# Retention's swapped halves and mLSTM's spread maximum: transfers on Pool's queue in place of matrix products

## What is computed

```python
x1, x2 = xf[..., :half], xf[..., half:]
return jnp.concatenate([x1 * cos - x2 * sin, x1 * sin + x2 * cos], axis=-1)
```

```python
m_t = jnp.maximum(jnp.max(Dlog, axis=2), inter)
W = jnp.exp(Dlog - m_t[:, :, None, :])
s = jnp.einsum('blhd,bshd->blsh', qc, kc) * W
```

## Time and profile before

| | |
|---|---|
| three runs | 1510.20, 1513.43 (median), 1519.79 us |
| span of the profiled execution | 1509.3 us |
| PE busy | 98% |
| DVE, ACT, POOL busy | 51%, 23%, 4% |
| PE clock granted | 0.9 or more of full in all 40 slices |
| DMA, mean | 199 GB/s; near full share in the last third (experts) |

### The profile page before, as it was taken

How to read it: one execution, slowest core, us unless ns; L and a number is a source line. 1 busy time by engine, 2 the same in 40 slices (tenths; PEclk the granted TensorE clock), 3 DMA queues, 4 the chain that set the end, 5 groups by cost and what they waited for, 6 DMA issues and landing times.

```text
span 1509.3 us, 40728 instructions
## 1 busy us (share of the span) xinstructions
PE 1479.3 (98%) x17933; PEld 1265.3 (84%) x17933; DVE 770.5 (51%) x1700; ACT 342.1 (23%) x855; POOL 56.2 (4%) x68
## 2 busy tenths in 40 slices
PE   9999999999999999999999999999999899999997
PEld 6899976887899999998899977887888787888654
DVE  6446756746665655657366667636662211221123
ACT  2314224222212212233224224123130000000001
POOL 1000010110000000000000010200010000000000
PEclk9999999999999999999999999999999999999999
DMA  8324435203544354256524353114879998999993
GB/s 349 115 88 164 155 139 133 85 25 93 210 154 153 131 188 144 81 207 225 201 100 176 144 150 111 45 44 125 330 314 359 407 360 304 361 355 366 363 385 106
DMA packets 64335, 299.84 MB, mean 199 GB/s; under 512 B 21840, under 2 KB 23568, under 8 KB 37664
## 3 DMA queue, kind: packets, MB, share of 16 engines
q1 hardware_dynamic: 50392, 268.10, 48.5%
q0 software_dynamic: 2944, 18.09, 3.1%
q10 hardware_dynamic: 10823, 11.05, 2.7%
HBM read 277.93 MB, written 19.28 MB: 197 GB/s over the span
## 4 chain that ended last, share of the span: by engine, by line
PE 93%; DVE 3%; DMA 2%; issue 1%; ACT 1%; SPq 0%; DVEq 0%; ACTq 0%
PE ps L2112 15%; PE ps L1250 12%; PE ps L1913 12%; PE ps L1713 9%; PE ps L2035 7%; PE ps L1720 5%; PE ps L1199 4%; PE ps L1825 4%; PE ps L2009 3%; PE ps L1212 2%; PE ps L1787 2%; PE ps L1569 2%; DMA ring<-in_mix 2%; PE ps L1946 2%; PE ps L1265 1%
## 5 line engine op out<-in xcount | busy, mean ns | idle before, releaser
L1713 PE MATMUL ps<-xn,ring 128*128 128x288 f32 x576 | 155.7, 414 | 0.4 <-ACT gate L2478 0.4
L1713 PEld LDWEIGHTS ps<-xn,ring 128*128 128x128 f32 x576 | 105.9, 190 | 37.2 <-issue 10.3
L2112 PE MATMUL ps<-arena 128*128 128x144 f32 x1028 | 133.4, 286 | 1.2 <-DVE arena L3649 1.2
L2112 PEld LDWEIGHTS ps<-arena 128*128 128x128 f32 x1028 | 129.3, 190 | 1.4 <-issue 1.4
L1913 PE MATMUL ps<-y_ml,arena 128*64 128x96 f32 (+4 forms) x2688 | 111.7, 244 | 11.5 <-issue 11.4
L1913 PEld LDWEIGHTS ps<-y_ml,arena 128*64 128x64 f32 x2688 | 109.2, 137 | 15.2 <-issue 15.1
L2035 PE MATMUL ps<-arena,mixed 128*32 128x256 f32 x2024 | 111.3, 380 | 0.0
L2035 PEld LDWEIGHTS ps<-arena,mixed 128*32 128x32 f32 x2024 | 65.0, 110 | 42.3 <-issue 0.2
L3573 DVE TENSOR_TENSOR mixed<-ps,mixed 128x96 f32<-128x96 f32 (+4 forms) x66 | 16.8, 254 | 130.3 <-PE ps L1913 130.1
L1913 PEld LDWEIGHTS ps<-y_ml,ring 128*64 128x64 f32 x1536 | 62.1, 137 | 4.8 <-issue 4.8
L1913 PE MATMUL ps<-y_ml,ring 128*64 128x96 f32 (+4 forms) x1536 | 64.3, 245 | 0.6 <-issue 0.6
(11 more groups left out here) (588 smaller groups left out, 2554.4 us busy)
## 6 DMA issues: line engine op xcount, KB each, us to landing
arena<-in_egu SPq DMA_DIRECT2D x56, 1024.0 KB, 7.4
ring<-in_mix SPq DMA_DIRECT2D x46, 1024.0 KB, 5.5
arena<-in_edown SPq DMA_DIRECT2D x40, 1024.0 KB, 7.3
ring<-in_mix SPq DMA_DIRECT2D x48, 768.0 KB, 4.2
ring<-in_egu SPq DMA_DIRECT2D x32, 1024.0 KB, 7.5
ring<-in_gu SPq DMA_DIRECT2D x14, 1024.0 KB, 4.8
arena<-in_gu SPq DMA_DIRECT2D x8, 1024.0 KB, 5.1
arena<-in_C POOLq DMA_DIRECT2D x2, 2048.0 KB, 7.9
```

Source lines behind the costliest of these rows:

```text
L1713: last = mm(ps[:, bank, 0:T], ring[:, s, P * k:P * k + P], xn[:, k, :], start=(k == 0), stop=(k == KT - 1))
L2112: last = mm(ps[:, dense_bank(side, product), 0:HALF], left, right, start=(k == 0 and product in (1, 2, 5)), stop=(k == n - 1), skip_group_ ...
```

## The change

The two kinds of product leave PE. The swapped halves come by four DMA transfers, each of 32 partitions with four tiles of 288 (`rqk` to `r_turned`), the running maximum by four DMA transfers that each read one partition's 256 numbers 128 times (`rows` to `row_copies`). All eight stand on Pool's queue, per layer. The copies of the rows wait for `lf_ok`; the swapped halves wait for the finished queries and keys and for PE's last head (`ml_nd` 4), since they are written over the mLSTM queries. n0 and the eight transfers share one semaphore: DVE waits for n0 and all four row copies at once, ahead of L2877, and for the four swaps ahead of the sine product, which is now one instruction of 1152 elements.

```diff
+        row_copies = at(19050, NH, TP)
+        r_turned = at(6570, 4, T)
+        ld_copies = sig("n0_and_copies_loaded", 144)
+        ld_n0_rows, ld_turned = Part(ld_copies, 79), Part(ld_copies, 143)
...
-                mm(ps[:, 4, 0:TP], picked_head(h), rows[0:NH, 1, 0:TP], start=True, stop=True)
                 mm(ps[:, 5, 0:TP], picked_head(h), rows[0:NH, 2, 0:TP], start=True, stop=True).then_inc(ml_bc.sem, 1)
...
-            def retention_rotate(l):
-                pe.wait_ge(*couple_added(l, 1, C12))
-                pe.wait_ge(*couple_copied(l, 1, 4))
-                for j in range(4):
-                    mm(ps[:, 4 + j, 0:T], C("swap", P), rqk[:, j, :], start=True, stop=True).then_inc(r_sw.sem, 1)
...
-                dve.wait_ge(ld_n0.sem, 16 * (l + 1))
+                dve.wait_ge(*ld_n0_rows(l))
...
-                STT(ml_W[:, 0:P], ps[:, 4, 0:P], g[0], C("causal_neg", P), ADD, ADD)
-                TSC(ml_W[:, P:TP], ps[:, 4, P:TP], g[0], None, ADD)
-                STT(ml_W[:, TP:PW], ps[:, 4, P:TP], g[1], C("causal_neg", P), ADD, ADD).then_inc(ml_wl.sem, 1)
+                STT(ml_W[:, 0:P], row_copies[:, h, 0:P], g[0], C("causal_neg", P), ADD, ADD)
+                TSC(ml_W[:, P:TP], row_copies[:, h, P:TP], g[0], None, ADD)
+                STT(ml_W[:, TP:PW], row_copies[:, h, P:TP], g[1], C("causal_neg", P), ADD, ADD).then_inc(ml_wl.sem, 1)
...
-                for j in range(4):
-                    dve.wait_ge(*r_sw(l, j + 1))
-                    last = TT(rt[:, j, :], ps[:, 4 + j, 0:T], C("sin", T), MUL)
-                link(last)
+                dve.wait_ge(*ld_turned(l))
+                link(TT(rt, r_turned, mid(C("sin", T), 4), MUL))
...
+                pool.wait_ge(*lf_ok(l))
+                for h in range(NH):
+                    pool.dma_start(row_copies[:, h, :], rows[h:h + 1, 1, 0:TP].unsqueeze(1).broadcast_to([1, P, TP])).then_inc(ld_copies.sem, 16)
+                pool.wait_ge(*couple_copied(l, 1, 4))
+                pool.wait_ge(*couple_added(l, 1, C12))
+                pool.wait_ge(*ml_nd(l, 4))
+                for first, other in ((0, 1), (1, 0), (2, 3), (3, 2)):
+                    pool.dma_start(r_turned[32 * first:32 * first + 32], rqk[32 * other:32 * other + 32])\
+                        .then_inc(ld_copies.sem, 16)
```

More of the change, by code:

```diff
@@ L796, in build @@
         ld_head, ld_con, ld_x, ld_lw, ld_hist = sig("ld_head"), sig("ld_con"), sig("ld_x"), sig("ld_lw"), sig("ld_hist")
-        ld_c0, ld_n0, ld_ret, ld_rw = sig("ld_c0"), sig("ld_n0"), sig("ld_ret"), sig("ld_rw")
+        ld_c0, ld_ret, ld_rw = sig("ld_c0"), sig("ld_ret"), sig("ld_rw")
+        ld_copies = sig("n0_and_copies_loaded", 144)
+        ld_n0_rows, ld_turned = Part(ld_copies, 79), Part(ld_copies, 143)
         st_ml, st_small, st_ret, st_rw, st_rws, st_y = (sig("st_ml"), sig("st_small"), sig("st_ret"), sig("st_rw"),
@@ L875, in hn_spread @@
             return hn_tensor.sem, 2 * q + 2
-        r_tensor, r_vector, r_scalar = sig("retention_tensor", 12), sig("retention_vector", 8), sig("retention_scalar", 7)
-        r_sw, r_kt, r_os, r_ot, r_sp, r_ss = (Part(r_tensor, k) for k in (0, 4, 7, 8, 9, 10))
+        r_tensor, r_vector, r_scalar = sig("retention_tensor", 8), sig("retention_vector", 8), sig("retention_scalar", 7)
+        r_kt, r_os, r_ot, r_sp, r_ss = (Part(r_tensor, k) for k in (0, 3, 4, 5, 6))
         r_qr, r_ktd, r_pw = (Part(r_vector, k) for k in (0, 1, 4))
@@ L2143, in _ @@
                 pe.wait_ge(*hn_used(l))
-                retention_rotate(l)
                 steps(l, AT_ROTATE, AT_RKEYS)
@@ L3774, in _ @@
                 pool.dma_start(C0, a["C"][l]).then_inc(ld_c0.sem, 16)
-                pool.dma_start(n0, a["n"][l]).then_inc(ld_n0.sem, 16)
+                pool.dma_start(n0, a["n"][l]).then_inc(ld_copies.sem, 16)
                 pool.dma_start(o["conv"][l], conv_out[:, :, :]).then_inc(st_small.sem, 16)
+                pool.wait_ge(*lf_ok(l))
[7 more added lines that the diff above has]
+                        .then_inc(ld_copies.sem, 16)
                 pool.wait_ge(*ml_sca(l, 2))
```

## The result

| | before | after |
|---|---|---|
| median of the runs on one chip, us | 1515.43 | 1539.72 |
| range, us | 1510.20 to 1519.79 | 1536.16 to 1541.85 |
| span of the profiled execution, us | 1509.3 | 1538.7 |

A forecast was written before the change was run, and what follows sets the result against it. PE, busy 98%, was taken as the bound: 4.3 us from heads plus 3.9 from rotations, 8.2, less 0.2 at the scores, gives 8.0; span 1509.3 becomes 1501.3, median 4.1 above, forecast 1505.4 us, range 1501 to 1515.

The forecast's parts named there:

- The term of 4.3: All eight heads: removing the maximum's spreading product from PE saves 0.54 us a head, 4.3 us in all.
- The rotation's 3.9 us: Retention: removing the rotation's four products from PE saves 1.94 us, twice, 3.9 us, which PE can take at once.
- Rival C: Heads: DVE's other work sets the pace, so only the rotations' 3.9 us come, 1509.5 us; chance 0.06.
- The tie at the first scores: Retention: DVE's L2994 ends at 175.74, PE's first scores would come at 175.77; 0.1 us lost a layer.
- The swapped halves: Retention: four 147 KB transfers in a row take 8 or 53 us; 8 taken, hidden before the sine product.
- The price of a row copy: Row copies before n0: 2 to 5.1 us each, four landing between 49 and 62 us in layer 0.
- upper choice: Row copies: 5.1 us each, 20.5 us for four, if one partition serves a sixteenth of 410 GB/s.
- Rival B: Both layers: one partition is slow to read, DVE waits at L2877; at 41 us a copy 1758 us; chance 0.12.
- The edit costs nothing, and what covers it is 33 us of stream on PE: Row copies: they land 12 us or more ahead of L2877, so DVE doesn't wait; cost nothing.
- rival A: Layer 1: slow copies hold up DMA engines, slabs and clearing land late; 7.8 us lost, 1513.2 us; chance 0.22.
- the forecast would fall if a copy passed 9.4 us: Row copies, layer 0: four have 37.6 us before PE stands, 9.4 us apiece; beyond that the forecast is wrong outright.
- in layer 0 the slabs have more room and I count nothing: Layer 0's slabs behind the row copies: more room than in layer 1, so no stall counted.

## Why the prediction was wrong, point by point

**What goes from PE: right in kind, a little large.** The products left as counted. But a head gained 0.45 us, not 0.54: over layer 0's heads, from behind the stand and its low clock to the product of L1287, the gain is 1.8 us: 11.1 late at 71.17, 9.3 at 166.52. The product of 71.17 before, and that of 157.20 after:

```profile
60.07 1.14 PE L1250 MATMUL ps<-mixed,ring 128*128 128x144 f32 x8
```

```profile
166.52 0.77 PE L1287 MATMUL ps<-arena,con 32*128 32x288 f32 x8
```

The spreading product that is left now has other neighbours, and the step from it to the scores' product is longer. A head of layer 1 before:

```profile
779.63 0.59 PE L1364 MATMUL ps<-arena,con 4*128 4x256 f32 x2
780.15 0.70 PE L1368 MATMUL ps<-arena 128*128 128x256 f32 x2
```

and the same head after:

```profile
784.03 0.69 PE L1367 MATMUL ps<-arena,con 4*128 4x256 f32 x2
784.65 0.70 PE L1371 MATMUL ps<-arena 128*128 128x256 f32 x2
```

Two spreading products took 0.54 and 0.52 us to the next start, the one that is left takes 0.62: 0.44 is gained a head, and the first of such a row costs 0.1 more, whichever it is. The term of 4.3 measures 3.6.

**The rotation's 3.9 us: not there.** The step that failed is "what follows the last head and the rotation is stream that depends on slabs and sums only, so PE can take the gain at once". The sums were the catch: they are DVE's, they stood behind its retention chain, and they had been just in time for a PE that was 1.94 us busy with the rotation. The lead was read for the values that the edit names (L2979, L2994) and not for the stream's own inputs. 0.4 us of 3.9 arrived; with the sums' order changed 3.8 did. Rival C named half a gain, but for the heads; it was the other half that failed.

**The tie at the first scores: right.** The working said 1.2 us of cover for the keys and a tie at the scores worth 0.1 us. In the change PE's stands hid it. Where they are gone, DVE's last product ends at 175.70, the scores start at 175.75, and the distance from keys to scores is 4.07 us where it was 3.97: 0.1.

**The swapped halves: right.** 2.3 to 4.5 us each, hidden.

**The price of a row copy: a little above the upper choice.** 5.5 us each against 2 to 5.1, 131072 / 5.5 = 23.8 GB/s; four landed at 63.4 where 62 was the late end. DVE didn't wait. Rival B didn't occur. The Trainium skill, "SBUF — State Buffer", section "Door 1: the DMA port swizzle", gives 27.6 GB/s for four neighbouring partitions; the trace's 23.8 for one partition is of that size. That the port behind the partition sets the pace is the Trainium skill's account; the run with 128 partitions as source shows only that it was the source.

**"The edit costs nothing, and what covers it is 33 us of stream on PE": the step that failed.** The sum asked only whether the consumer of the copies has time. It left to rival A the question whom the copies keep waiting while they have it: the stream that is said to cover them lives on slabs that pass through the same 16 engines. Even the sentence that the forecast would fall if a copy passed 9.4 us was about the consumer alone; at 5.5 us apiece it fell.

**Rival A was the mechanism, nearly four times too small.** It had the engines take turns between a copy and a slab and priced it at 5.1 us a slab and 7.8 us in all, in layer 1 alone. Measured, 29.6: slabs landed in 20 and 28 us where they had taken 4.7 and 9.4, with stands of 8.2 and 16.6. Three of its terms were mis-sized. First, the turn: it took one row of 1 KB between two of a slab; a packet held four rows and kept an engine for 2.1 us. The Trainium skill, "DMA: Bandwidth & Descriptors", section "Queues, rings and completion order", has an engine drain a whole packet, of several descriptors, before it turns to another queue; the counts above (63 to 53) agree with the turns, and the size of the packet is what was overlooked. Second, only one packet of the slab moved in the first 6.7 us after its issue in layer 0, and none for some 19 in layer 1, where the clearing of `slots` shared the turns; A had none of this. Third, "in layer 0 the slabs have more room and I count nothing": the slab issued at 45.29 was wanted at 57.2, 12 us later, and before it took 4.7, so its room was 7 us and the loss 15.3. The row that tells it, the issue of that slab, is not among those that the prediction works from. The 4.4 us of low clock behind the stands was in no rival.

So the chances went wrong in one place: 0.22 for A was fair for its kind, but its price, bounded only at one row per turn, put it at no change. With four rows to a turn a slab takes up to 4 x 5.1 = 20.4 us more; less its room, 7.2 in layer 0 and 2.3 in layer 1, that is 31 us in both layers, an estimate made afterwards, against stands of 24.8 measured.

**What stays open.** What delays a slab's first packet behind the copies was not tried. In the clear of 45.3 to 52 us 42 data packets of the copies went by, 2.6 for each engine, and one of the slab; in the version on ACT's queue the first slab packet came over 8 us after its issue at 44.9. Whether engines had taken the copies' work in advance, no row shows. Nor does a run tell one partition from one address, or place the stretches at the low clock in which PE was busy.

## What to carry to other kernels

A transfer has two prices: the time until it lands, which its consumer must cover, and the time that it keeps the DMA engines from others, which every load behind it pays; read the second off packets and share of the queues, not off bytes. A small thing to be spread to all partitions should be read from many partitions or from HBM: 4 KB out and 512 KB back took 5.6 us in layer 0, where four times 128 reads of one partition took 22. And when work leaves the engine that sets the pace, list everything that feeds it in the next few microseconds, the inputs of the filler work too, and move what is late next along with the edit.

## What the runs showed of the hardware that was not expected

- The 16 engines together read one partition at 23.8 GB/s, and were 93 to 95% busy meanwhile: the slowness of a source shows as busy time of all engines, not of one.
- Packets of Pool's queue held 4 KB (four rows, 2.1 us each out of one partition), those of ACT's queue one row (0.51 us).
- With ACT as issuer, the issue of one such transfer took up to 5.6 us of ACT's time; on Pool 0.54 us.
- PE stood 8.2 and 16.6 us, and the first 3.62 us of work behind it took 5.90 and 5.76, some 2.2 us more. Behind the short stand of 0.60 us in the run with half the length it took 3.69, next to nothing more.
- The clock also fell to its lower level with PE busy: granted 0.68 from 755 to 760 us before, which cost 1.4 us.
